# Prompt attention of a hybrid decoder step: both key-value groups at once on halves of the array, with the softmax weights scaled before the value product

## The reference, cut to what matters

```
N_HEADS = 8; N_KV = 2; HEAD_DIM = 64; GROUP = 4        # 4 query heads for each key-value group
def one_block(item):                                    # 128 queries each: two blocks (qt = 0, 1)
    s_c = einsum('qgrd,cgd->qgrc', qi, k_cmp[b]) * scale        # 15 compressed keys
    p_c = masked_softmax(s_c, cmp_end <= qp)
    o_c = einsum('qgrc,cgd->qgrd', p_c, v_cmp[b])
    ...
    o_s = einsum('qgrm,qgmd->qgrd', p_s, v_g)                   # selected keys; all 4 blocks in the prompt
    o_w = einsum('qgrk,kgd->qgrd', p_w, wb[:, 1])               # window: all earlier keys in the prompt
g_nsa = sigmoid(nsa_g.reshape(bsz, t, N_HEADS, 3))
o_nsa = einsum('bthk,btkhd->bthd', g_nsa, o_br)                 # gated sum of the three branches
```

## Time and profile before

| | |
|---|---|
| median of 3 runs | 2351.76 us (2342.68 to 2353.7) |
| the profiled execution, its own time | 2357.69 us |
| its span | 2356.0 us |
| mean granted TensorE clock | 0.937 of 2.4 GHz |
| PE busy | 2161.1 us (92%) |
| DVE, ACT, POOL busy | 446.6, 336.6, 175.4 us |

### The profile page before, as it was taken

The page is one execution under the profiler, slowest core; times in us unless marked ns, Lnnn a source line. Parts: engine busy times, 40 slices in busy tenths (PEclk is TensorE's granted clock), DMA queues, the critical chain, the costliest instruction groups (busy, mean ns, idle before and its releaser), DMA issues.

```text
span 2356.0 us, 41787 instructions
## 1 busy us (share of the span) xinstructions
PE 2161.1 (92%) x17242; PEld 1337.5 (57%) x17242; DVE 446.6 (19%) x1128; ACT 336.6 (14%) x869; POOL 175.4 (7%) x327
## 2 busy tenths in 40 slices
PE   7888869999999989886899979999999999999995
PEld 5777647667777777774676663434343354343332
DVE  1412326421000014232453230000000000000001
ACT  2124212111000011341121110001010101010010
POOL 2222122200000000212100000000000000000000
PEclk8897989899999988878998979999999999999998
DMA  6543245353333322423332329999999899999996
GB/s 259 184 160 121 85 140 182 135 206 117 127 141 128 140 90 79 148 76 133 120 125 100 118 89 376 378 419 380 414 379 421 341 401 371 421 378 417 380 405 231
DMA packets 85249, 548.53 MB, mean 233 GB/s; under 512 B 12704, under 2 KB 12864, under 8 KB 26208
## 3 DMA queue, kind: packets, MB, share of 16 engines
q1 hardware_dynamic: 65568, 475.74, 51.6%
q0 software_dynamic: 17616, 63.65, 8.1%
q10 hardware_dynamic: 1904, 6.69, 0.8%
HBM read 532.61 MB, written 21.74 MB: 235 GB/s over the span
## 4 chain that ended last, share of the span: by engine, by line
PE 49%; issue 43%; ACT 3%; DVE 2%; POOLq 2%; POOL 1%; DMA 1%; SPq 0%; DVEq 0%
PE bank L426 36%; PE bank L529 3%; POOLq L1067 1%; PE bank L592 1%; PE bank L568 1%; PE bank L580 1%; PE bank L442 1%; ACT phase_region L1254 1%; PE bank L460 1%; PE bank L790 1%; ACT L1254 1%; ACT phase_region L1140 1%; DVE xn L1442 0%; PE bank L434 0%; PE bank L485 0%
## 5 line engine op out<-in xcount | busy, mean ns | idle before, releaser
L918 PE MATMUL bank<-wring,phase_region 128*32 128x512 f32 (+2 forms) x9728 | 873.5, 521 | 11.8 <-ACT phase_region L1140 7.1
L426 PE MATMUL bank<-xn,wring 128*128 128x288 f32 x2496 | 655.8, 424 | 3.3 <-DVE xn L1442 3.3
L918 PEld LDWEIGHTS bank<-wring,phase_region 128*32 128x32 f32 x9728 | 326.0, 110 | 554.6 <-issue 484.1
L426 PEld LDWEIGHTS bank<-xn,wring 128*128 128x128 f32 x2496 | 493.9, 200 | 148.1 <-issue 7.8
L1140 ACT ACTIVATE phase_region<-bank 128x512 f32<-128x512 f32 (+14 forms) x258 | 94.8, 441 | 566.1 <-PE bank L885 212.0
L426 PE MATMUL bank<-phase_region,wring 128*128 128x288 f32 x608 | 148.2, 407 | 3.1 <-DVE mark L1430 2.5
L426 PEld LDWEIGHTS bank<-phase_region,wring 128*128 128x128 f32 x608 | 115.3, 190 | 36.0 <-DVE mark L1430 3.4
L1926 DVE TENSOR_TENSOR tmp<-phase_region,bank 128x512 f32<-128x512 f32 x32 | 22.0, 688 | 543.6 <-PE bank L918 542.9
L1384 ACT ACTIVATE phase_region<-bank 128x512 f32<-128x512 f32 (+1 forms) x48 | 25.2, 543 | 539.3 <-PE bank L918 539.3
L1072 POOL DMA_DIRECT2D pages<-in_slc_pages x128 | 68.7, 536 | 269.9 <-issue 269.9
L1069 POOL DMA_DIRECT2D pages<-in_cmp_pages x128 | 68.7, 537 | 201.1 <-issue 201.1
(11 more groups left out here) (322 smaller groups left out, 1351.1 us busy)
## 6 DMA issues: line engine op xcount, KB each, us to landing
wring<-in_wstream SPq DMA_DIRECT2D x449, 1024.0 KB, 7.4
pages<-in_cmp_pages POOLq DMA_DIRECT2D x128, 128.0 KB, 2.4
pages<-in_slc_pages POOLq DMA_DIRECT2D x128, 128.0 KB, 2.3
out_win_keep<-in_win_rows POOLq DMA_DIRECT2D x2, 4064.0 KB, 27.7
y_rows<-phase_region ACTq DMA_DIRECT2D x17, 384.0 KB, 5.3
pages<-in_win_kT POOLq DMA_DIRECT2D x4, 1024.0 KB, 5.2
pages<-in_win_v POOLq DMA_DIRECT2D x16, 256.0 KB, 5.8
phase_region<-in_ssm_in POOLq DMA_DIRECT2D x2, 1024.0 KB, 7.1
```

Source lines behind the costliest of these rows:

```text
L426: mm = nc.tensor.matmul(ps[:, 0:width], wb, rhs(k), start=(k == 0), stop=(k == n - 1))
L918: mm = nc.tensor.matmul(ps[QT * q:QT * q + QT, 0:n], lhsT, w, start=start, stop=stop)
```

## The change

The 12 units become 6 pairs: a pair is one query block and one branch, for both groups. The scores of the two groups alternate, group 0 on rows 0 to 63 of the array and group 1 on rows 64 to 127, into different banks. The weights are multiplied by gate over sum on DVE before they are turned (`pair_norm`), which is a new step between the exponentials and the transposes. The value product has the values as the stationary operand, 64 columns for each group (column half g of the array), and streams 512 columns of turned weights, so that the result comes out in feature order. DVE adds it into `oN` at once. `otok`, its four transposes per query block and their copies are gone. The two score buffers hold one group each instead of alternate units, so that the softmax of the next pair may overwrite them only when the transposes of this pair are done; there are now four buffers of turned weights instead of two. `compress(1)` comes after two pairs and the scores of a third, and the fillers are spread anew.

```diff
@@ -37,8 +37,10 @@
 NREST = len(REST)
 EARLY = 3
-UNIT_REST = [None if n in (3, 6, 9) else EARLY + n - n // 3 for n in range(12)]
-CMP1_UNIT = 3
+CMP1_RESTS = 3
+PAIRS = [(qt, br) for qt in range(2) for br in range(3)]
+CMP1_PAIR = 2
+PAIR_RESTS = [(3, 4), (5,), (6, 7), (8,), (9, 10), (11,)]
 MERGE = [(br, m) for br in (0, 2, 1) for m in range(KD)]
         qkv = ra(NQKV, T)
         vtok = ra(3, 3, P)
-        otok = ra(2, GRP, NKV, HD)
         rp = Region(scratch)
         S_p = [rp(1024), rp(1024)]
-        PT_p = rp(2, 4 * P)
-        otmp = rp(GRP, HD)
+        PT_p = [rp(2, 4 * P), rp(2, 4 * P)]
         rs_ = Region(scratch)
@@ -550,69 +552,57 @@
                 nc.tensor.transpose(ps[0:NCP, 0:P], vcTp[:, 0:NCP], ident).then_inc(done, 1)
                 pe.wait_ge(S["vtok_ready"], l + 1)
...
+                def pair_scores(m):
+                    qt, br = PAIRS[m]
+                    w, nkc = pair_width(m)
+                    nk = w * nkc
+                    per = GRP if br == 0 else 512 // nk
+                    for part in range(GRP // per):
+                        banks = [bank(("S", l, m, g, part)) for g in range(NKV)]
+                        for i in range(per):
+                            for g, (ps, done) in enumerate(banks):
+                                gd = slice(HD * g, HD * g + HD)
+                                keys = kcTp[gd, 0:NCP] if br == 0 else qkv[gd, 4 + br, 0:nk]
+                                mm = nc.tensor.matmul(ps[:, i * nk:(i + 1) * nk], qkv[gd, part * per + i, qt * P:qt * P + P], keys,
+                                                      start=True, stop=True)
+                                if i == per - 1:
+                                    mm.then_inc(done, 1)
+
+                def pair_transposes(m):
+                    w, nkc = pair_width(m)
+                    for g in range(NKV):
+                        s = S_p[g][:, 0:GRP * w * nkc].rearrange("p (r k) -> p r k", r=GRP)
+                        pe.wait_ge(S["norm_ready"], 12 * l + 2 * m + g + 1)
+                        for kc in range(nkc):
+                            ps, done = bank(("T", l, m, g, kc))
+                            for r in range(GRP):
+                                mm = nc.tensor.transpose(ps[0:w, r * P:(r + 1) * P], s[:, r, kc * w:(kc + 1) * w], ident)
+                            mm.then_inc(done, 1)
+
+                def pair_out(m):
+                    br = PAIRS[m][1]
+                    w, nkc = pair_width(m)
+                    pe.wait_ge(S["pt_ready"], 6 * l + m + 1)
+                    ps, done = bank(("O", l, m))
                     for kc in range(nkc):
...
+                        for g in range(NKV):
+                            gc = slice(HD * g, HD * g + HD)
+                            v = vcp[0:w, gc] if br == 0 else vtok[:, kc, br, gc]
+                            mm = nc.tensor.matmul(ps[gc, 0:512], v, PT_p[g][0:w, kc, :], start=(kc == 0), stop=(kc == nkc - 1))
                     mm.then_inc(done, 1)
                 pe.wait_ge(S["vc_ready"], 3 * l + 1)
...
+                pair_scores(0)
+                for m in range(6):
+                    if m == CMP1_PAIR:
                         compress(1)
...
+                    if m < 5:
+                        pair_scores(m + 1)
+                    rest(PAIR_RESTS[m][0])
+                    pair_transposes(m)
+                    for i in PAIR_RESTS[m][1:]:
+                        rest(i)
+                    pair_out(m)
                 pe.wait_ge(S["qbd_ready"], l + 1)
                 for hf in range(2):
@@ -1245,27 +1235,32 @@
                 evac(("vcp", l), vcp[0:NCP, :], P, NCP)
                 signal("vc_ready")
...
+                def pair_exp(m):
+                    w, nkc = pair_width(m)
+                    for g in range(NKV):
+                        s = S_p[g][:, 0:GRP * w * nkc].rearrange("p (r k) -> p r k", r=GRP)
+                        act.wait_ge(S["smax"], 12 * l + 2 * m + g + 1)
+                        for r in range(GRP):
+                            e = A.activation(s[:, r, :], s[:, r, :], ACT.Exp, bias=mx[:, g, r:r + 1],
+                                             accum_out=ssum[:, g, r:r + 1])
+                        e.then_inc(S["exp_ready"], 1)
+
+                pair_exp(0)
+                for m in range(6):
+                    w, nkc = pair_width(m)
+                    if m == CMP1_PAIR:
                         for kind, k in ((0, 0), (0, 1), (1, 0), (1, 1)):
                             evac_cmp(("cmp", l, 1, kind, k), kvT[1][kind][:, 2 * k:2 * k + 2, :])
                         signal("vcT_ready")
...
+                    rest(PAIR_RESTS[m][0])
+                    for g in range(NKV):
+                        for kc in range(nkc):
+                            evac(("T", l, m, g, kc), PT_p[g][0:w, kc, :], 512, w)
                     signal("pt_ready")
...
+                    if m < 5:
+                        pair_exp(m + 1)
+                    for i in PAIR_RESTS[m][1:]:
+                        rest(i)
                 for hf in range(2):
                     it = 2 * l + hf
@@ -1468,43 +1463,54 @@
                 last.then_inc(S["kxk_ready"], 1)
...
+                def pair_softmax(m):
+                    qt, br = PAIRS[m]
+                    w, nkc = pair_width(m)
+                    w *= nkc
                     if br == 0:
                         mask = C("cmp_mask")[:, qt * NCP:(qt + 1) * NCP]
                     else:
                         mask = C(("causal0", "causal1")[qt])
...
+                    parts = nkc
                     nr = GRP // parts
...
+                    for g in range(NKV):
+                        s = S_p[g][:, 0:GRP * w].rearrange("p (r k) -> p r k", r=GRP)
+                        if m:
+                            dve.wait_ge(*filled(("T", l, m - 1, g, pair_width(m - 1)[1] - 1)))
+                        for part in range(parts):
+                            dve.wait_ge(*filled(("S", l, m, g, part)))
+                            ps = bank_of(("S", l, m, g, part))
+                            V.scalar_tensor_tensor(s[:, part * nr:(part + 1) * nr, :],
+                                                   ps[:, 0:nr * w].rearrange("p (r k) -> p r k", r=nr), HD ** -0.5,
+                                                   bc(mask, 1, nr), ALU.mult, ALU.add).then_inc(free(("S", l, m, g, part)), 1)
+                        dve.wait_ge(*released(("S", l, m, g, parts - 1)))
+                        V.tensor_reduce(mx[:, g, :], s, AX.X, ALU.max, negate=True).then_inc(S["smax"], 1)
+
+                def pair_norm(m):
+                    qt, br = PAIRS[m]
+                    w, nkc = pair_width(m)
+                    w *= nkc
                     dve.wait_ge(S["gates_ready"], l + 1)
...
+                    for g in range(NKV):
+                        s = S_p[g][:, 0:GRP * w].rearrange("p (r k) -> p r k", r=GRP)
+                        dve.wait_ge(S["exp_ready"], 12 * l + 2 * m + g + 1)
+                        link(V.reciprocal(rsum, ssum[:, g, :]))
+                        gate = gates[:, qt, g * 12:(g + 1) * 12].rearrange("p (r k) -> p r k", k=3)[:, :, br]
+                        link(V.tensor_tensor(coef, rsum, gate, ALU.mult))
+                        if br == 0:
+                            link(V.tensor_scalar(coef, coef, C("cmp_any")[:, qt:qt + 1], None, ALU.mult))
+                        V.tensor_tensor(s, s, bc(coef, 2, w), ALU.mult).then_inc(S["norm_ready"], 1)
+
+                def pair_out(m):
+                    qt, br = PAIRS[m]
+                    dve.wait_ge(*filled(("O", l, m)))
+                    src = bank_of(("O", l, m))[:, 0:512].rearrange("p (r q) -> p r q", r=GRP)
+                    dst = oN[:, :, qt * P:(qt + 1) * P]
                     if br == 0:
...
+                        V.tensor_copy(dst, src).then_inc(free(("O", l, m)), 1)
+                    else:
+                        dve.wait_ge(*released(("O", l, m - 1)))
+                        V.tensor_tensor(dst, dst, src, ALU.add).then_inc(free(("O", l, m)), 1)
                 def rest(i):
@@ -1533,14 +1539,15 @@
                                          sc_st[:, j, :].rearrange("p (b k) -> p b k", b=NB))
                 link(last)
...
+                pair_softmax(0)
+                for m in range(6):
+                    pair_norm(m)
+                    rest(PAIR_RESTS[m][0])
+                    if m < 5:
+                        pair_softmax(m + 1)
+                    for i in PAIR_RESTS[m][1:]:
+                        rest(i)
+                    pair_out(m)
                 link(V.memset(qbd, 0.0))
                 for g in range(NKV):
```

## The result

The changed kernel took 2278.68 us (median of 4 runs, 2275.6 to 2287.96), the kernel before in the same session 2352.65. The ratio is 0.9694, 95% interval 0.9671 to 0.9717: 74 us faster. The prediction had 2303 with a range from 2288 to 2327. In a later session the ratio was 0.9716 (0.9696 to 0.9736).

A forecast was written before the change was run, and what follows sets the result against it. PE, busy 92% of the span, was taken as the bound. Each stretch after the second compression takes 48.5 + 8.5 = 57 us, both 114 instead of 165.2, 51 us less: 2303 us, range 2288 to 2327.

The forecast's parts named there:

- `compress(1)` set by POOL's fetches: Ahead of the second compression: POOL's last page fetch sets its start, which stays as before, at most 0.5 us later.
- The sum at full clock: From the second compression to the sample attention: PE work and waits per layer add up to 48.5 us before clock loss.
- six fillers: After the second compression: six at 4.04 us each, 24.2 us at full clock.
- three score pairs: After the second compression: 5.35 us if row halves run together; rival without overlap 4.6 us more per layer, 2313, chance 0.14.
- four transposes: After the second compression: as many as before, 1.3 + 1.15 + 2.1 + 2.1 = 6.65 us.
- four value products: After the second compression: records of 512 columns, column halves overlapping, 5.7 us; without overlap 5.6 us more.
- waits for copies and banks: After the second compression: PE waits 0.8 and 0.9 us for turned weights' copies, 1.0 and 2.2 us for banks.
- end: Before the sample attention: DVE's last addition, clearing and filling the sample queries, with hand-overs 1.75 us.
- The scaling: Between exponentials and transposes: hidden with about 1 us to spare; rival that it or banks hold PE, 2323, chance 0.13.
- The clock: After the second compression: 30% at half level, 8.5 us lost; rival of half level throughout, 2367, chance 0.04.
- Switching tiling modes: Fillers beside half-array products: no visible gap; by a draining rule at 0.1 us per switch, 2.4 us worse.
- Gain swallowed by page fetches: Sample attention: rival that second-half fetches don't move or the 30 us slack is used up; 2350, chance 0.04.

The follow-up runs named there:

- e12_no_scaling: Changed kernel without DVE's multiplication of the exponentials by their factors (result not the reference's); 2279.63 us, ratio 0.9711 to the kernel before.
- e9_after_again: Changed kernel run again unaltered, in a later session; 2280.68 us, ratio 0.9716 to the kernel before.
- e4_before_waits_filled: Kernel before, with 22 unused 288-column products per layer put where PE would have waited; 2317.75 us, ratio 0.9865.
- e5_waits_back: Changed kernel with the filler between scores and transposes moved behind the transposes, same PE work; 2282.31 us, ratio 0.9726 to the kernel before.
- e3_values_moving: Changed kernel with the value product turned back: weights stationary, 64 columns of values streamed; 2293.34 us, ratio 0.9766 to the kernel before.
- e6_compression_later: Changed kernel with the second compression put one filler later, into the wait for pages; 2275.82 us, ratio 0.9699 to the kernel before.

## Why the prediction was right in its mechanism and wrong in its size

**`compress(1)` set by POOL's fetches: right.** It started 1.9 us after the last fetch was issued in layer 1, the first stretches were 26.17 and 26.38 us long, and PE idled ahead of it for 3.06 and 6.55 us. All starts lie earlier than the forecast 153.8 and 961.8 only because what is ahead of them came earlier.

**The sum at full clock: right, term by term.** Layer 0 ran at 1.00 and can be read straight against it (time from one start to the next, idle time taken out; all in us):

| term | predicted | layer 0 after |
|---|---|---|
| six fillers | 24.2 | 23.98 |
| three score pairs | 5.35 | 4.86 |
| four transposes | 6.65 | 5.96 |
| four value products | 5.7 | 5.89 |
| waits for copies and banks | 1.7 + 3.2 | 1.70 + 3.14 |
| end | 1.75 | 1.65 |
| sum | 48.5 | 47.18 |

The scores and transposes are a little shorter, since a following instruction starts before the shown end of the one ahead of it. The overlap, which was inferred from records that use row and column halves in turn, held in full. The bank waits, read off the order of DVE's work, came within 0.1 us.

**The scaling: right, but closer than it looks.** It had 1 us to spare by the prediction. The last scaling ahead of the fifth pair's transposes, in layer 0 and in layer 1 of the changed kernel:

```profile
188.09 1.23 DVE L1502 TENSOR_TENSOR phase_region<-phase_region 128x1024 f32<-128x1024 f32 x1
956.60 1.23 DVE L1502 TENSOR_TENSOR phase_region<-phase_region 128x1024 f32<-128x1024 f32 x1
```

It was ready 2.1 us ahead of the transposes in layer 1 (957.83 against 959.89), but PE came 1.6 us late there, at the half level. In layer 0, at full clock, it was 0.4 us (189.32 against 189.73). Taking the scaling away changed nothing (`e12_no_scaling`), but PE was late by the half level in both layers of that run and of the one beside it.

**The clock: the step that failed.** "I take 30% at the half level, 8.5 us of loss in 57; the bounds are 14% (4 us) and 50% (15 us)." Measured were a clock of 1.00 and 0.96 (0.93 and 0.96 in `e9_after_again`, a loss of 3.1 and 1.6), which is a loss of 0 and 1.6 us: 48.73 less the 47.1 of the same work at full clock. All of them lie below the lower bound of 4 us. The waits of after that I counted, 6.65 us, were right (6.49 and 6.40). What was wrong is the step from them to a share of the half level. A share of waiting time is no measure of it: at full clock, 9.4 us of waits in 66.5 were 14% of the stretch before, and 6.4 in 47.2 are 14% after. The one lost 32 us in two stretches, the other 1.6 (4.7 in `e9_after_again`). `e4_before_waits_filled` shows that the loss goes when long products fill the waits, and `e5_waits_back` that the order of the same work counts. Between fillers the kernel before had up to 13.2 us of short products and waits (1000.39 to 1013.60 in layer 1, part of it at the half level), and the changed one has up to 7.2. I take that for the reason, but no run varied it by itself, and `e3_values_moving` lost clock at a place where a wait was gone. So why the clock came back almost whole is argued and not shown; that it did, and what it was worth, is measured.

So the 69.3 us of the two stretches are 32.3 us of clock less the 1.6 that are left, 30.7, and 38.6 us of work and waits. The forecast had 51 in all. Its clock term was 15.4 us too high (17.0 against 1.6) and its sum 2.7 (97.0 against 94.3). The upper bound was taken beside a rule of "TensorE: Matmul & The Clock Gate" of the Trainium skill (Part 4: transposes don't count as activity in the same way). By it the stretch should have lost its clock again. Its 48 transpose records in 47.18 us are as dense as the 64 of before in 66.5 us at full clock, and it ran at 1.00 in layer 0; so did all 64 in `e4_before_waits_filled`. These traces don't bear out that the transposes set the loss.

**Switching tiling modes: the prediction misread its rows.** It saw no gap between full-array and half-array products. The single records show one at full clock. Within a filler a record starts 0.242 us after the one ahead. From the last record of a filler to a value product on the full array it is 0.242 us too (kernel before, 957.68), but to one on column halves it is 0.336 us (changed kernel, 941.49). On the way back, from row-half scores or a column-half product into a filler, its second record starts 0.346 us after the first, and 0.245 behind transposes. So each change costs about 0.1 us. That is the size which the prediction tried for the rule on draining under Key Properties in "TensorEngine Tiling (Array Packing)" of the Trainium skill; the traces agree that a change has a price, but don't tell a drain from another cause. The count was wrong as well: the scores of two units are now one run, so a third stretch has 10 changes between full, row-half, column-half and 15-row products, where it had 20. As an estimate from these spacings, the change saves 1 us in each third stretch, where the prediction weighed 1.2 us more per layer.

**Gain swallowed by page fetches: right to drop it.** The waits for pages are 17.09 and 6.99 us, against 17.17 and 6.71. The slack of 30 us is used up, though: the last fetch of the first half starts at 982.11, 1.7 us behind the start of the sample attention, and lands 5.5 us later. What saved the gain is that PE reads these pages only at 997.37, about 10 us after that; before it was 49.

**What stays open.** For the profiled pair the forecast of 2307 was 31 us too long: 18.1 of it are the stretches, and the other 12.8 us lie outside them, where the forecast had put nothing. By the medians it was 24.3 us, since the profiled execution before was slower than its median and the one after faster. The first scores of layer 0 lay at 128.50 and 125.80 before, at 120.29 and 122.83 in the two profiles of the changed kernel, and at 120.6 to 128.06 in its variants: that is scatter in good part. The way from the sample attention of layer 0 to the scores of layer 1 took 683.5 and 683.3 us before and 677.6 in both profiles of the changed kernel, but 677.6 to 683.8 in variants that alter nothing there. Its granted clock differs by 0.01, and PE is busy 632.9 us of it before and 628.0 after. What sets that wasn't tried.

## What to carry to other kernels

When the profile shows a low granted clock beside many short waits of PE, price the two together. Fill the waits with long unused products in the kernel as it is: one run tells what the clock costs, and here that was 30 us, some 40% of what the change gained. And when a change removes waits, don't scale the clock loss by the waiting time that is left: at the same 14% of waits two stretches lost 32 us or 2 to 5.

Where an engine waits for page fetches that are issued one by one, work ahead of that wait is nearly free up to the landing of the last page, and the fetches, not the products, decide when the stretch ends. Look at the landing too: with more work moved ahead (`e6_compression_later`) it came up to 2 us later.

## What the runs showed of the hardware that was not expected

- Adding 44 unused products to the kernel before made it 29.9 us faster (ratio 0.9865, 0.9849 to 0.9882), with the granted clock of the stretches going from 0.79 to 1.00. The 22 per layer are 288 columns each, and stand where PE waited.
- Products on the two row halves run together even if all of one half's products of a bank are issued ahead of the other's: 2.10 us for 16 records of 256 columns, against 2.00 issued in alternation and 1.99 for the 8 records of one half alone. With 15 columns it matters more: 1.53 against 1.07 us.
- Of two profiles of the same changed kernel, one ran layer 0's stretch at 1.00 (47.18 us) and one at 0.93 (50.26 us), with the same waits at the same places to 0.1 us. So a clock term scatters by some 3 us per stretch between executions of one kernel.
- A change between a full-array product and one on half of the rows or columns costs about 0.1 us at full clock: 0.336 us from the last record of a filler to a column-half product, where 0.242 us lie between records of the full array.
